# Experts' gate and up products as seven half-size products in two column groups of TensorE

## What is computed

```python
aff = jax.nn.softmax((h @ w_router).astype(F32), -1)
gate, idx = lax.top_k(jnp.swapaxes(aff, 1, 2), cap)      # cap = 128
xe = h[bidx, idx]
he = jax.nn.silu(jnp.einsum('becd,edf->becf', xe, w1)) * jnp.einsum('becd,edf->becf', xe, w3)
ye = jnp.einsum('becf,efd->becd', he, w2) * gate[..., None].astype(h.dtype)
return jnp.zeros_like(h).at[bidx, idx].add(ye)
```

## Time and profile before

| | |
|---|---|
| median of 3 runs | 4019.66 us (4019.06 to 4022.24) |
| profiled execution, span from first to last instruction | 4017.8 us; it stands 1.9 us below the median of the runs |
| TensorE busy | 3714.7 us, 92% |
| VectorE, ScalarE, GpSimd busy | 38%, 18%, 11% |
| gate and up products (1508), TensorE | 1128.9 us |
| down products (1494), TensorE | 562.6 us |
| granted TensorE clock, mean | 0.965 |

### The profile page before, as it was taken

One profiled execution on the slowest core, in us unless ns is written; L12 is line 12 of the kernel. 1 busy time (PEld: TensorE's weight loads), 2 busy tenths in 40 slices (PEclk: granted clock), 3 DMA queues, 4 the chain that ended last, 5 costly groups with the idle time before them and its releaser, 6 DMA issues. The chain is left out here.

```text
span 4017.8 us, 48174 instructions
## 1 busy us (share of the span) xinstructions
PE 3714.7 (92%) x19742; PEld 2081.2 (52%) x19742; DVE 1530.6 (38%) x2609; ACT 704.6 (18%) x1506; POOL 444.3 (11%) x500
## 2 busy tenths in 40 slices
PE   7999899987989999999999998999977898869996
PEld 3444488874434444444444444644455898534442
DVE  5656379983810000000000000555166678550001
ACT  2000022210111000010000100412125443112112
POOL 0000000003200000000000000200031776000110
PEclk9999999998989999999999999999988999989998
DMA  7563133216599898888888885412102100219996
GB/s 285 217 257 151 66 125 127 116 42 242 204 341 357 314 311 305 309 310 307 308 308 308 308 300 179 163 49 74 38 0 77 46 4 4 96 53 382 337 332 202
DMA packets 286345, 799.44 MB, mean 199 GB/s; under 512 B 14920, under 2 KB 22096, under 8 KB 271312
## 3 DMA queue, kind: packets, MB, share of 16 engines
q1 hardware_dynamic: 268160, 720.05, 49.5%
q0 software_dynamic: 17280, 74.59, 5.8%
q10 hardware_dynamic: 720, 2.17, 0.2%
HBM read 709.60 MB, written 87.16 MB: 198 GB/s over the span
## 5 line engine op out<-in xcount | busy, mean ns | idle before, releaser
L1508 PE MATMUL banks<-moe_ring,moe_xeT 128*128 128x512 f32 x2560 | 1128.9, 594 | 7.0 <-ACT moe_xeT L1549 7.0
L1508 PEld LDWEIGHTS banks<-moe_ring,moe_xeT 128*128 128x128 f32 x2560 | 481.7, 191 | 584.1 <-issue 581.3
L1604 DVE TENSOR_TENSOR moe_hid<-moe_silu,banks 128x512 f32<-128x512 f32 x80 | 55.0, 688 | 1421.6 <-PE banks L1508 1421.6
L1494 PE MATMUL banks<-moe_ring,moe_hidT 128*128 128x512 f32 x1280 | 562.6, 592 | 1.7 <-DVE moe_ye L1590 1.0
L1494 PEld LDWEIGHTS banks<-moe_ring,moe_hidT 128*128 128x128 f32 x1280 | 240.8, 190 | 293.4 <-issue 291.3
L1789 PE MATMUL banks<-hT,w_in_ring 128*128 128x512 f32 (+3 forms) x976 | 364.0, 535 | 1.9 <-ACT hT L1850 1.1
L512 PE MATMUL banks<-hT,w_in_ring 128*128 128x512 f32 x768 | 339.3, 596 | 1.7 <-PEq L212 1.7
L1789 PEld LDWEIGHTS banks<-hT,w_in_ring 128*128 128x128 f32 (+1 forms) x976 | 183.1, 188 | 181.0 <-issue 170.3
L1568 ACT ACTIVATE moe_silu<-banks 128x512 f32<-128x512 f32 x80 | 47.8, 597 | 1226.3 <-PE banks L1508 1226.2
L512 PEld LDWEIGHTS banks<-hT,w_in_ring 128*128 128x128 f32 x768 | 142.8, 190 | 185.7 <-issue 176.2
L733 PE MATMUL banks<-taps_in,dft 128*128 128x256 f32 x768 | 168.2, 379 | 0.0
(11 more groups left out here) (451 smaller groups left out, 4006.7 us busy)
## 6 DMA issues: line engine op xcount, KB each, us to landing
moe_ring<-d_wg SPq DMA_DIRECT2D x80, 2048.0 KB, 9.4
moe_ring<-d_wu SPq DMA_DIRECT2D x80, 2048.0 KB, 8.3
moe_ring<-d_wd SPq DMA_DIRECT2D x80, 2048.0 KB, 8.3
w_in_ring<-d_w_in SPq DMA_DIRECT2D x9, 2048.0 KB, 10.4
x_normed<-d_mod_w SPq DMA_DIRECT2D x8, 2048.0 KB, 12.5
d_taps<-dft SPq DMA_DIRECT2D x8, 2048.0 KB, 7.4
taps_in<-d_taps SPq DMA_DIRECT2D x8, 2048.0 KB, 9.3
w_in_ring<-d_hy_w_in SPq DMA_DIRECT2D x6, 2048.0 KB, 8.6
```

Source lines behind the costliest of these rows:

```text
L1494: last = nc.tensor.matmul(m.ps[:, Y_BANK + h, :], hidT[:, c, i * P:(i + 1) * P], down(c)[:, i, h * BANK:(h + 1) * BANK], start=(fc == 0 an ...
L1508: last = nc.tensor.matmul(m.ps[:, 2 * kind + c, :], xeT[:, k, :], up(c, kind)[:, k, :], start=(k == 0), stop=(k == KT - 1))
L1604: nc.vector.tensor_tensor(hid[:, j % 2, :], sg[:, j % 2, :], m.ps[:, 2 + j % 2, :], ALU.mult).then_inc(s.hid, 1)
```

## The change

A unit's gate and up products are computed by Strassen's scheme in Winograd's form. The 128 tokens are cut into two halves of 64, the depth into even and odd tiles, the 512 columns into a left and a right half. Seven products of halves, 64 tokens by 4 depth tiles by 256 columns, take the place of eight. Each runs for gate and up at once: gate's output goes to partitions 0-63 and up's to 64-127 of the same bank, so the stationary tile has 64 columns and two column groups of the array alternate (`product`). VectorE makes four sums of weights per unit, one unit ahead (`weight_sums`: three into wsums, one over the raw weights), four sums of tokens per expert (`token_sums`), and from the seven results the four quarters (`combine`); ScalarE copies five of the seven out of PSUM first (`part`). Silu and the multiplication work on 64 partitions (`activate`).

Of raw gate and up weights two units are kept, one in a buffer of its own and one in m.X, which is free in this stage. They are loaded by depth halves, four transfers of 1 MB. Of down weights there is now one buffer instead of two, and hid and hidT have one buffer as well. The token transposes of the next expert stand in two sets, behind the first and behind the fourth product of an expert's last unit.

```diff
+HK = KT // 2
+HN = EW // 2
+HT = P // 2
+LOW, HIGH = slice(0, HT), slice(HT, P)
+LEFT, RIGHT = slice(0, HN), slice(HN, EW)
...
+    PRODUCTS, COPIES, SUMS = 7, 3, 4
...
-        nc.sbuf_tensor(f"{name}_ring", [P, 2, 3, 8 * EW], F32) as ring,
+        nc.sbuf_tensor(f"{name}_raw", [P, 4 * HK * EW], F32) as raw0,
+        nc.sbuf_tensor(f"{name}_wsums", [P, 3, 2 * HK, HN], F32) as wsum,
+        nc.sbuf_tensor(f"{name}_down", [P, EW // P, D], F32) as wd,
-        nc.sbuf_tensor(f"{name}_xeT", [P, KT, P], F32) as xeT,
-        nc.sbuf_tensor(f"{name}_silu", [P, 2, EW], F32) as sg,
-        nc.sbuf_tensor(f"{name}_hid", [P, 2, EW], F32) as hid,
-        nc.sbuf_tensor(f"{name}_hidT", [P, 2, EW], F32) as hidT,
+        nc.sbuf_tensor(f"{name}_xeT", [P, 2, KT, P], F32) as xeT,
+        nc.sbuf_tensor(f"{name}_xsums", [P, 2, 4, HK, HT], F32) as xs,
+        nc.sbuf_tensor(f"{name}_parts", [P, 5, HN], F32) as pp,
+        nc.sbuf_tensor(f"{name}_silu", [P, 4, HN], F32) as sg,
+        nc.sbuf_tensor(f"{name}_hid", [P, EW], F32) as hid,
+        nc.sbuf_tensor(f"{name}_hidT", [P, EW], F32) as hidT,
-        up = lambda c, kind: ring[:, c, kind, :].rearrange("p (k n) -> p k n", k=KT)
...
+        raw = [x.rearrange("p (a k n) -> p a k n", a=2, n=EW) for x in (raw0[:], m.X[:].rearrange("p t d -> p (t d)"))]
+        T_BANK, Y_BANK, ROWS_BANK = 4, 5, 7
+        PAIR_BANK, P65_BANK, P7_BANK, P34_BANK = 0, 1, 2, 3
...
+            def load_half(j, a, e):
+                cols = slice(j % nf * EW, (j % nf + 1) * EW)
+                for kind, w in enumerate((d_gate, d_up)):
+                    sp.dma_start(raw[j % 2][:, a, kind * HK:(kind + 1) * HK, :], pick(w, e)[:, a:KT:2, cols]
+                                 ).then_inc(raw_in[j % 2][a], 16)
+
+            def load_down(fc, e):
+                sp.dma_start(wd[:], pick(d_down, e)[:, fc * (EW // P):(fc + 1) * (EW // P), :]).then_inc(s.wd, 16)
 
             def load(turn):
                 first = isinstance(turn, int) and turn == 0
-                at = [settled(sp, turn * EU + eu) for eu in range(EU)]
-                before = None if first else settled(sp, turn * EU - 1)
-                pick = lambda w, e: w[e] if isinstance(e, int) else w[ds(e, 1)].rearrange("a p k n -> (a p) k n")
+                at = {eu: settled(sp, turn * EU + eu) for eu in range(0 if first else -2 // nf, EU)}
                 for j in range(FU):
-                    eu, fc, c = j // nf, j % nf, j % 2
-                    n = turn * FU + j
-                    cols = slice(fc * EW, (fc + 1) * EW)
-                    if not first or j >= 2:
-                        sp.wait_ge(s.g_mm, n - 1)
-                    sp.dma_start(up(c, 0), pick(d_gate, at[eu])[:, :, cols]).then_inc(wg_in[c], 16)
-                    if first and j == 0:
+                    e, fresh = at[j // nf], first and j < 2
+                    if not fresh:
+                        sp.wait_ge(s.p_mm, turn * (PRODUCTS * FU) + PRODUCTS * (j - 2) + 5)
+                    load_half(j, 0, e)
+                    if fresh and j == 0:
                         sp.wait_ge(gathered[0], 16)
-                    if not first or j >= 2:
-                        sp.wait_ge(s.u_mm, n - 1)
-                    sp.dma_start(up(c, 1), pick(d_up, at[eu])[:, :, cols]).then_inc(wu_in[c], 16)
-                    if j:
-                        load_down(pick(d_down, at[(j - 1) // nf]), j - 1, n - 1)
-                    elif not first:
-                        load_down(pick(d_down, before), FU - 1, n - 1)
+                    if not fresh:
+                        sp.wait_ge(s.p_mm, turn * (PRODUCTS * FU) + PRODUCTS * (j - 2) + 7)
+                    load_half(j, 1, e)
+                    if not fresh:
+                        if not first or j > 2:
+                            sp.wait_ge(s.d_mm, turn * FU + j - 2)
+                        load_down((j - 2) % nf, at[(j - 2) // nf])
...
+            for n in (N - 2, N - 1):
+                sp.wait_ge(s.d_mm, n)
+                load_down(n % nf, n // nf)
...
+            def product(bank, at, tokens, weights):
+                for k in range(HK):
+                    for kind, out in ((0, LOW), (1, HIGH)):
+                        last = nc.tensor.matmul(m.ps[out, bank, at], tokens(k), weights(kind * HK + k),
+                                                start=(k == 0), stop=(k == HK - 1))
+                last.then_inc(s.p_mm, 1)
...
+                for j in range(FU):
+                    eu, fc, n = j // nf, j % nf, turn * FU + j
+                    c, copied, sums = j % 2, turn * (COPIES * FU) + COPIES * j, turn * (SUMS * FU) + SUMS * j
+                    following = next_expert(turn, j, final)
+                    x = lambda a, tok: lambda k: xeT[:, eu, 2 * k + a, tok]
+                    xsum = lambda i: lambda k: xs[:, eu, i - 1, k, :]
+                    w = lambda a, cols: lambda k: raw[c][:, a, k, cols]
+                    t = lambda i: lambda k: wsum[:, i, k, :]
+                    if fc == 0:
+                        pe.wait_ge(s.s_all, turn * EU + eu + 1)
+                    pe.wait_ge(s.t, sums + 1)
+                    if started or j:
+                        pe.wait_ge(s.copied, copied - 2)
+                    product(P65_BANK, RIGHT, xsum(1), t(0))
+                    if following:
+                        rows(*following, 0)
+                    pe.wait_ge(s.t, sums + 3)
+                    product(P65_BANK, LEFT, xsum(2), t(1))
+                    pe.wait_ge(s.t, sums + 4)
+                    if started or j:
+                        pe.wait_ge(s.c_all, n)
+                    product(P34_BANK, RIGHT, x(1, HIGH), t(2))
+                    if started or j:
+                        turned(n - 1)
+                        pe.wait_ge(s.copied, copied)
+                    product(PAIR_BANK, RIGHT, x(0, LOW), w(0, LEFT))
+                    if following:
+                        rows(*following, 1)
+                    product(P7_BANK, LEFT, xsum(3), w(0, RIGHT))
+                    product(PAIR_BANK, LEFT, x(1, LOW), w(1, LEFT))
+                    product(P34_BANK, LEFT, xsum(4), w(1, RIGHT))
+                    if started or j:
+                        back((j - 1) % nf, n - 1, turn * EU + (j - 1) // nf)
...
+            def part(to, bank, done):
+                act.wait_ge(s.p_mm, done)
+                w = to.stop - to.start
+                nc.scalar.copy(pp[:, to, :], m.ps[:, bank, 0:w * HN].rearrange("p (a n) -> p a n", a=w)).then_inc(s.copied, 1)
...
+                    if started or j:
+                        act.wait_ge(s.hid, 2 * n)
+                    part(slice(2, 4), P65_BANK, products + 2)
+                    if started or j:
+                        turned(n - 1)
+                    if following:
+                        rows(*following, 1)
+                    part(slice(4, 5), P7_BANK, products + 5)
+                    part(slice(0, 2), PAIR_BANK, products + 6)
+                    act.wait_ge(s.c22, n + 1)
+                    act.wait_ge(s.c_all, n + 1)
+                    nc.scalar.activation(sg[HIGH], pp[LOW, 0:4, :], ACT.Silu).then_inc(s.act, 1)
...
+            def token_sums(turn, eu):
+                e = turn * EU + eu
+                v.wait_ge(s.xt, e * 2 + 2)
+                a = lambda deep, tok: xeT[:, eu, deep:KT:2, tok]
+                s1, s2, s3, s4 = (xs[:, eu, i] for i in range(4))
+                nc.vector.tensor_tensor(s1, a(0, HIGH), a(1, HIGH), ALU.add).then_inc(s.s1, 1)
+                nc.vector.tensor_tensor(s3, a(0, LOW), a(0, HIGH), ALU.subtract)
+                v.wait_ge(s.s1, e + 1)
+                nc.vector.tensor_tensor(s2, s1, a(0, LOW), ALU.subtract).then_inc(s.s2, 1)
+                v.wait_ge(s.s2, e + 1)
+                nc.vector.tensor_tensor(s4, a(1, LOW), s2, ALU.subtract).then_inc(s.s_all, 1)
+
+            def weight_sums(turn, j):
+                c, n = j % 2, turn * FU + j
+                loads = turn * (FU // 2 * 32) + (j // 2 + 1) * 32
+                done, sums = turn * (PRODUCTS * FU) + PRODUCTS * (j - 1), turn * (SUMS * FU) + SUMS * j
+                b11, b12 = raw[c][:, 0, :, LEFT], raw[c][:, 0, :, RIGHT]
+                b21, b22 = raw[c][:, 1, :, LEFT], raw[c][:, 1, :, RIGHT]
+                t1, t2, t4 = (wsum[:, i] for i in range(3))
+                v.wait_ge(raw_in[c][0], loads)
+                if after_first(n):
+                    v.wait_ge(s.p_mm, done + 1)
+                nc.vector.tensor_tensor(t1, b12, b11, ALU.subtract).then_inc(s.t, 1)
+                v.wait_ge(raw_in[c][1], loads)
+                v.wait_ge(s.t, sums + 1)
+                nc.vector.tensor_tensor(b12, b22, b12, ALU.subtract).then_inc(s.t, 1)
+                if after_first(n):
+                    v.wait_ge(s.p_mm, done + 2)
+                v.wait_ge(s.t, sums + 2)
+                nc.vector.tensor_tensor(t2, b22, t1, ALU.subtract).then_inc(s.t, 1)
+                if after_first(n):
```

(35 more changed lines are left out.)

167 lines of the change are left out of this document (58 added, 109 removed).

## The result

The changed kernel takes 4050.14 us, the median of four runs (4044.38 to 4056.47); before, run beside it, 4019.36 (4017.43 to 4022.24). The ratio is 1.0076 with a 95% interval of 1.0061 to 1.009: slower by 0.8%. The prediction said 4009 us; the time lies inside its range of 3968 to 4060, on the other side of no change.

What follows compares the result with a forecast made beforehand. TensorE's own work was taken as the bound in both experts stages, DMA close behind in the second. Terms -130.4 + 49.6 + 16.8 + 34.4 + 19.3 gave -10.3 us, hence 4009 us; range 3968 to 4060.

Steps and rivals of the forecast that it cites:

- products: Gate and up products of each unit: 56 pairs at 0.216 us, 1.63 us less per unit, -130.4 us over 80 units.
- changes of width: TensorE going from half width to full and back twice per unit, for hid's transposes and down: 0.62 us per unit, +49.6 us.
- token transposes: Next expert's token transposes, now two sets inside half-width products, 15 experts in each of 2 stages: +16.8 us.
- starts: Start of both experts stages: first product also waits for weight and token sums, unit 0's down weights land late; +34.4 us.
- ends: End of both experts stages: last down weights are issued only when the down product before has ended; +19.3 us.
- transfers: Weight loads: five issues instead of three for the same 6.29 MB, down weights needed 13.2 us after issue; costed at nothing.
- Rival (c): Single down buffer: down weights land over 13.2 us after issue, TensorE waits; 0.5 us per unit is +40, 4049 us; chance 0.17.
- (a): Rival: width round trips cost little, as the next loads are ready; all gone, -66.4 us, 3943 us; chance 0.14.
- (b): Rival: two weight loads of 64 columns don't overlap, pairs go at 0.26 us; +197, 4206 us; chance 0.07.
- (d): Rival: the two column groups don't overlap at all in the products; +968, 4977 us; chance 0.02.

## Why the prediction was wrong

| step | forecast, us | measured in the profiled execution, us |
|---|---|---|
| products, changes of width, token transposes | -130.4 + 49.6 + 16.8 = -64.0 | -61.7 |
| starts | +34.4 | +36.0 |
| ends | +19.3 | +20.9 |
| jump of TensorE's loop | none | +20.4 |
| input weights in front of turn 1 | none | +10.5 |
| small waits for down weights | none | +5.6 |
| outside the two stages | none | -3.1 |
| sum | -10.3 | +28.6 |

First row measured: 1.00 us in each of 50 units and 0.39 in 30 (21.91 before, 21.52 now). Starts: what is left of each stage's difference in length, 23.7 and 12.3; in the first stage product 1 is 16.2 later against the stage's own start, the down wait is 5.1 and the half clock behind it 2.8. Ends: 24.7 from next to last down to the end, as forecast, and 27.1 in the second stage, where it was 15.6 before. Jump: 117.6 - 100.2 in the boundary units and 3.0 in the units behind them. Input weights: units 6 and 7, 30.19 and 21.91 in place of 21.52 and 20.04.

The three terms with a place in the sum were right within 6 us together. The steps that failed are the jump and the transfers, both put at nothing; they make up 36.5 of the 38.9 us by which the sum was off. In detail:

- **The change of code length wasn't in the list of parts.** The prediction counted the instructions that each engine gains as time, and not as length of TensorE's program. By the traces its body in the first stage grew from 907 to 2227 instructions, since seven products of halves with two groups are 112 MATMULs of 256 columns in place of 32 of 512. The kernel before had both kinds of evidence: its jump of 0.215 us, and not one instruction packet in a stretch of repeated turns. It is the largest of the errors, 20.4 us by the trace, and the small waits (5.6 us) went with it. Without the jump the kernel is level with the one before (0.9995), and only with the transfers mended as well is it faster, so the missing 39 us are not this step's alone.
- **The transfers were put at nothing.** "SyncE has an idle queue" was read from steady turns. Between turns 0 and 1 the queue holds 4 MB for the next stage. The kernel before has the same 4 MB there and no long unit. With two down buffers the down weights could be asked for a unit earlier; with one, issue in time is all that covers them (argued from the code: no kernel with two buffers beside the new scheme was run). Rival (c) named the single buffer as the mechanism that ends slower, but priced it evenly at 0.5 us per unit. In steady state it is nothing (the kernel with jump and transfers mended has no such wait at all), and at five known places it is 3.5 to 9.9 us each. The rival was right in kind, and wrong in where. The landing time in the first stage was taken from before, 7.9 us in the median, and is 11.1.
- **Starts and ends** were sized well. In the first stage the wait for unit 0's down weights was 5.1 and not 1.3, with half clock behind it: they are issued behind both raw halves of unit 2, at 1160.43, and land 17.0 us later. With them requested in front of those halves the wait is gone.

Of the rivals, (a) is out: a round trip costs 0.30 us beside half-width products too, and the unit of 20.04 us is 0.63 above its work of 12.10, 6.87 and 0.44, where the forecast had 0.62. That agrees with the Trainium skill (TensorEngine Tiling (Array Packing), "Key Properties"), by which a change of mode drains TensorE. (b) and (d) are out: pairs go at 0.216 us. By the share that the Trainium skill gives for three column tiles (TensorE: Matmul & The Clock Gate, "Measured speedup vs the span model") a pair would have been 0.272 us, an estimate; the trace does not agree: two groups of 64 run at 2.0 times the speed of one. For four of 32 the prediction said four times; its own 1.86 us are 3.7 times and the router's 0.219 us 3.9, still above that share.

## What to carry to other kernels

Count what a change does to the length of a loop body, per engine, as well as to its busy time, and look at the jump and at the instruction packets of the trace before: they show whether the body fits. When a buffer becomes single, check the first, the last and every irregular place in the queue of its loads, not the steady turns. And where several waits stand in a row, the whole time tells too little of what removing one is worth, so read its place in the trace: the moved input weights took 10.5 us from units 6 and 7 and five boundary units grew by 5.3; the moved transposes shorten units by 33 us in all, and alone gave 15.

## What was unexpected of the hardware

- TensorE's jump back took 0.21 to 0.25 us with bodies of 255 to 1761 instructions and 6.1 to 8.1 us with 1843, 2227 and 2241. Down's 16 matmuls, 6.87 us, hide most of it, and in the changed kernel a second stall, 2.2 to 2.9 us from one matmul to the next, comes inside the second product behind it. With 2241 in the second stage the jump of 6.70 us stood beside down and cost 0.14 us (7.20 from down to the next product, in place of 7.06), with no second stall; with 1843 there was none either, and no gap over 1.8 us. So the visible price differs from jump to jump.
- Straight code of 8 turns has no such stall, though it brings nearly as many instruction packets (197 in place of 210 in the whole program).
- Two column groups of 64 run at full overlap when they alternate; eight of one and then eight of the other still overlap in part, 2.79 us in place of 1.73 or 3.46.
- Behind an idle stretch of 5.1 us in front of down, down ran at half clock for its first 5.7 us (the granted clock is 0.50 from 1176.5 to 1183.3), so the wait cost 7.9.
